# The late modulation's pieces of the head passes on GpSimd instead of VectorE

## The reference

```python
def _adaln(cvec, w_mod, b_mod):
    m = jax.nn.silu(cvec) @ w_mod + b_mod                # (2048) @ (2048, 6 * 2048)
    return jnp.split(m[..., None, :], 6, axis=-1)        # shift, scale, gate of mixer and FFN

def _block(s, mod, s0_f, s0_b, p):
    sh_a, sc_a, g_a, sh_f, sc_f, g_f = mod
    h = _rmsnorm(s, p['norm_pre_mix']) * (1.0 + sc_a) + sh_a
    out, s_f, s_b = _mixer(h, s0_f, s0_b, p)             # 8 heads of gated DeltaNet | Hyena
    s = s + g_a * _rmsnorm(out, p['norm_post_mix'])
    h = _rmsnorm(s, p['norm_pre_ffn']) * (1.0 + sc_f) + sh_f
    ff = (jax.nn.silu(h @ p['w_gate']) * (h @ p['w_up'])) @ p['w_down']
    return s + g_f * _rmsnorm(ff, p['norm_post_ffn']), s_f, s_b
```

## Time and profile before

| | us |
|---|---|
| median of three runs | 1667.03 |
| the runs | 1659.72, 1667.03, 1667.48 |
| the profiled execution | 1659.05 |
| its span, from first to last instruction | 1657.4 |
| TensorE busy | 1608.8 |
| VectorE busy | 1148.5 |
| ScalarE busy | 769.1 |
| GpSimd busy | 117.1 |

### The profile page before, as it was taken

The page is one execution under the profiler, slowest core; times in us unless marked ns, Lnnn a source line. Parts: engine busy times, 40 slices in busy tenths (PEclk is TensorE's granted clock), DMA queues, the critical chain, the costliest instruction groups (busy, mean ns, idle before and its releaser), DMA issues.

```text
span 1657.4 us, 26938 instructions
## 1 busy us (share of the span) xinstructions
PE 1608.8 (97%) x10074; PEld 1398.9 (84%) x10074; DVE 1148.5 (69%) x1699; ACT 769.1 (46%) x1285; POOL 117.1 (7%) x214
## 2 busy tenths in 40 slices
PE   6998999999999999999998999999999999999997
PEld 2356999999998998999998888888888888888886
DVE  4726889899898997776777555555555555655665
ACT  3436465564646556433346444444444444343331
POOL 1001010110101010000110000000000000111110
PEclk9998999999999999999999999999999999999999
DMA  9996354453544545324993444554455446877872
GB/s 367 414 356 237 121 166 153 134 179 121 172 138 132 171 133 185 102 102 154 342 330 140 152 182 175 200 202 175 180 202 198 172 187 242 283 247 253 281 250 93
DMA packets 83067, 332.59 MB, mean 201 GB/s; under 512 B 8073, under 2 KB 24538, under 8 KB 56668
## 3 DMA queue, kind: packets, MB, share of 16 engines
q1 hardware_dynamic: 63168, 262.44, 43.1%
q0 software_dynamic: 19408, 67.77, 12.3%
q10 hardware_dynamic: 396, 1.10, 0.2%
HBM read 327.09 MB, written 4.19 MB: 200 GB/s over the span
## 4 chain that ended last, share of the span: by engine, by line
PE 82%; DMA 8%; DVE 5%; ACT 2%; DVEq 1%; issue 1%; SPq 0%; ACTq 0%
PE g L490 10%; PE o L490 10%; PE o L483 7%; PE o L484 7%; PE o L485 7%; PE g L491 5%; PE o L491 5%; DMA w_mod_tile_o<-in_w_mod_t 4%; DMA w_mod_raw<-in_w_mod_t 4%; PE g L566 2%; PE o L497 2%; PE g L497 2%; PE o L499 2%; PE g L499 2%; PE g L498 2%; PE g L577 2%
## 5 line engine op out<-in xcount | busy, mean ns | idle before, releaser
L464 DVE TENSOR_TENSOR w_lo<-w_raw,w_hi 128x2048 fp32r<-128x2048 f32 x202 | 462.4, 2289 | 201.8 <-ACT w_hi L459 201.4
L459 ACT CAST w_hi<-w_raw 128x2048 fp32r<-128x2048 f32 x203 | 388.0, 1911 | 219.3 <-PE o L499 73.9
L483 PE MATMUL o<-h_hi,w_hi 128*128 128x256 f32 (+1 forms) x880 | 291.6, 331 | 2.3 <-ACT hy_x L1232 1.3
L485 PE MATMUL o<-h_hi,w_lo 128*128 128x256 f32 (+1 forms) x880 | 275.3, 313 | 0.0
L484 PE MATMUL o<-h_lo,w_hi 128*128 128x256 f32 (+1 forms) x880 | 275.1, 313 | 0.0
L490 PE MATMUL g<-h_hi_lo,w_hi 128*128 128x512 f32 x704 | 245.0, 394 | 0.0
L490 PE MATMUL o<-h_hi_lo,w_hi 128*128 128x512 f32 x688 | 240.5, 394 | 2.0 <-DVE h_hi_lo L2036 2.0
L491 PE MATMUL g<-h_hi_lo,w_lo 128*128 128x256 f32 x704 | 195.0, 277 | 0.0
L491 PE MATMUL o<-h_hi_lo,w_lo 128*128 128x256 f32 x688 | 190.6, 277 | 0.0
L483 PEld LDWEIGHTS o<-h_hi,w_hi 128*128 128x128 f32 x880 | 168.0, 191 | 13.6 <-issue 6.9
L485 PEld LDWEIGHTS o<-h_hi,w_lo 128*128 128x128 f32 x880 | 167.4, 190 | 10.4
(11 more groups left out here) (393 smaller groups left out, 2820.1 us busy)
## 6 DMA issues: line engine op xcount, KB each, us to landing
w_raw<-in_w_ff_t SPq DMA_DIRECT2D x88, 1024.0 KB, 6.1
w_raw<-in_w_heads_t SPq DMA_DIRECT2D x56, 1024.0 KB, 4.9
w_mod_raw<-in_w_mod_t SPq DMA_DIRECT2D x32, 1024.0 KB, 11.1
w_raw<-in_w_down_t SPq DMA_DIRECT2D x32, 1024.0 KB, 6.8
w_mod_piece_h<-in_w_mod_t POOLq DMA_DIRECT2D x112, 256.0 KB, 3.6
w_raw<-in_w_out_t SPq DMA_DIRECT2D x16, 1024.0 KB, 8.4
w_mod_tile_o<-in_w_mod_t POOLq DMA_DIRECT2D x16, 1024.0 KB, 9.8
w_mod_piece_d<-in_w_mod_t POOLq DMA_DIRECT2D x64, 256.0 KB, 5.9
```

Source lines behind the costliest of these rows:

```text
L459: e.copy(whi[p.split[j]][:], raw[p.raw[j]][:]).then_inc(hi_ready, 1)
L464: e.tensor_tensor(wlo[p.split[j]][:], raw[p.raw[j]][:], whi[p.split[j]][:].bitcast(F32), ALU.subtract).then_inc(lo_ready, 1)
L483: e.matmul(o, a, xh, start=first, stop=False)
L485: return e.matmul(o, b, xh, start=False, stop=last)
```

## The change

VectorE's `head_pieces` and its 16 places in the order of a pass go. GpSimd's `head_load` becomes `head_chunk`: it waits until the column sum of the pass before is done (`macc_used`), then goes through the pieces, issuing the load of piece n and computing piece n - 2. VectorE's one instruction (multiply by a column and add) becomes two on GpSimd: `tensor_scalar` in place in the piece's buffer, then `tensor_tensor` into `w_mod_sum_h`, with a drain before each. The loop over pass pairs on GpSimd is written out as straight code. The pieces of the later stages stay on VectorE, and the orders of TensorE, ScalarE and SyncE are the same.

```diff
--- before.py
+++ after.py
@@ -1503,13 +1503,6 @@
             else:
                 last = v.tensor_scalar(acc, raw_, c, None, mulv)
             last.then_inc(mtile_done, 1)
-
-        def head_pieces(v, pairs, u, k0, k1):
-
-            for k in range(k0, k1):
-                v.drain()
-                v.wait_ge(mpiece_landed[piece_slot(u, k)], piece_landed(pairs, u, k))
-                mod_piece(v, k, mpiece_h[piece_slot(u, k)][:], macc_h[:])
 
         def out_pieces(v, t0, t1):
 
@@ -1887,9 +1880,6 @@
                     if not (isinstance(g, int) and g == 0):
                         scan_dve_(v, g - 1, 1 - u, step)
 
-                def pc(k0, k1):
-                    head_pieces(v, 0 if p is Hf else i + 1 - u, u, k0, k1)
-
                 def mod():
                     modulation(v, g + 5, 1, g + 1, F[1])
 
@@ -1898,12 +1888,12 @@
                         v.wait_ge(rows_t, 9)
                         v.tensor_tensor(modc[:, 0, 48:52], F[1][:, 0:8:2], bmod[:, 48:52], addv)
 
-                inv("hv"); pc(0, 1); scan("v0"); pc(1, 3); late_row(); rp(); scan("S0"); pc(3, 4); scan("v1"); pc(4, 5); scan("w1"); pc(5, 6)
-                inv("nr"); scan("S1"); pc(6, 7); inv("kt"); inv("bb"); scan("v2"); pc(7, 9); scan("w2"); cc(); pc(9, 10); inv("A")
-                scan("v3"); inv("U0"); pc(10, 11); inv("D1"); inv("ag"); scan("S2"); inv("M1"); pc(11, 12); inv("DT1"); scan("w3")
+                inv("hv"); scan("v0"); late_row(); rp(); scan("S0"); scan("v1"); scan("w1")
+                inv("nr"); scan("S1"); inv("kt"); inv("bb"); scan("v2"); scan("w2"); cc(); inv("A")
+                scan("v3"); inv("U0"); inv("D1"); inv("ag"); scan("S2"); inv("M1"); inv("DT1"); scan("w3")
                 cv(0); inv("M2"); inv("DT2"); re(0); inv("D2"); scan("nb"); inv("M3"); inv("DT3"); re(1); at_(); inv("D3")
-                inv("M4"); cv(1); inv("DT4"); re(2); cv(2); inv("D4"); sm(0); pc(12, 13); inv("M5"); inv("DT5"); re(3); pc(13, 14)
-                inv("D5"); sm(1); inv("M6"); pc(14, 15); inv("DT6"); pc(15, 16); cv(4); re(4); inv("D6"); sm(2); scan("mix")
+                inv("M4"); cv(1); inv("DT4"); re(2); cv(2); inv("D4"); sm(0); inv("M5"); inv("DT5"); re(3)
+                inv("D5"); sm(1); inv("M6"); inv("DT6"); cv(4); re(4); inv("D6"); sm(2); scan("mix")
                 cv(5); mod(); zm(); inv("Z")
                 v.drain()
 
@@ -2111,12 +2101,27 @@
             def piece(n, k):
                 return A["w_mod_t"][4 * n + k // 4][:, k % 4 * 512:(k % 4 + 1) * 512]
 
-            def head_load(h, u):
-
-                for k in range(16):
-                    wait_count(g, mtile_done, 16 * h + k + 1 - piece_gap(u, k))
-                    s = piece_slot(u, k)
-                    g.dma_start(mpiece_h[s][:], piece(13 + h, k)).then_inc(mpiece_landed[s], 16)
+            def head_chunk(h, u, pairs):
+
+                wait_count(g, macc_used, h)
+                for n in range(18):
+                    if n < 16:
+                        wait_count(g, mtile_done, 16 * h + n + 1 - piece_gap(u, n))
+                        s = piece_slot(u, n)
+                        g.dma_start(mpiece_h[s][:], piece(13 + h, n)).then_inc(mpiece_landed[s], 16)
+                    k = n - 2
+                    if k >= 0:
+                        s = piece_slot(u, k)
+                        g.drain()
+                        g.wait_ge(mpiece_landed[s], piece_landed(pairs, u, k))
+                        c = cvec[:, 2, 2 * k:2 * k + 1]
+                        if k:
+                            g.tensor_scalar(mpiece_h[s][:], mpiece_h[s][:], c, None, ALU.mult)
+                            g.drain()
+                            last = g.tensor_tensor(macc_h[:], macc_h[:], mpiece_h[s][:], ALU.add)
+                        else:
+                            last = g.tensor_scalar(macc_h[:], mpiece_h[s][:], c, None, ALU.mult)
+                        last.then_inc(mtile_done, 1)
 
             g.memset(fm[FW:P, 0], 0.0)
             g.memset(fw[FW:P, 3 * FW:], 0.0).then_inc(filt_pad, 1)
@@ -2144,10 +2149,10 @@
             g.dma_start(lev[:].bitcast(F32), A["c_lev"]).then_inc(lev_in, 16)
             g.wait_ge(first_used, 4)
             g.wait_ge(w_used, st.tile(H0, 0, 1) + 1)
-            head_load(0, 0)
-            with g.Fori(0, H.iters) as i:
-                head_load(2 * i + 1, 1)
-                head_load(2 * i + 2, 0)
+            head_chunk(0, 0, 0)
+            for i in range(H.iters):
+                head_chunk(2 * i + 1, 1, i)
+                head_chunk(2 * i + 2, 0, i + 1)
             w_ov(g, HEADS - 1, "mix")
             by_pairs = A["w_mod_t"].rearrange("(c g) p (h f) -> g h p c f", g=4, h=2)
             for t in range(16):
```

## The result

The changed kernel takes 1964.82 us (median of four runs, 1951.64 to 1970.37) against 1666.3 before: ratio 1.1797, 95% interval 1.1756 to 1.1838. It is slower, as forecast, but by 299 us and not by 50, and outside the range. Ratios leave out one execution of 5670.66 us, in `early_seven` further down; the median of its nine runs has it in. The page after, to set against the earlier trace rows: span, busy time and share by engine, and the granted clock in 40 slices.

A forecast was written before the change was run, and what follows sets the result against it. TensorE was taken to bound the head passes. VectorE's loss of 9.2 us, less 0.75 and 1.3, gave 7.2 us a pass; seven passes, 50 us, on 1659.05 made 1709 us, range 1655 to 1760.

The forecast's parts named there:

- A piece then takes 3.9 us: GpSimd's time per piece in the head passes: 3.2 us, plus 0.7 us of waiting for VectorE's two-tile instructions.
- two more steps of 0.30: In GpSimd's time per piece: two steps from a semaphore to the start, 0.30 us each, beside issue and arithmetic.
- The scaling: GpSimd's in-place scaling of a 512-element piece: two memory streams, between 0.45 and 0.90 us, taken as 0.68.
- the addition: GpSimd's addition of a piece into the sum: three memory streams, 0.75 to 1.35 us, taken as 1.05.
- rival C: Head passes become as long as GpSimd's chain, the column sum waiting for the sixteenth piece: up to 1761 us; chance 0.17.
- threshold of 4.2 us: Time per piece in a head pass, (70.57 - 3.6) / 16, from which the column sum waits for GpSimd's sixteenth piece.
- other sign: What would show rival C in a pass besides TensorE idle before L512: GpSimd has no gaps.
- the forecast's own high end: Late stretch of a pass: 4.4 us a piece, 15.2 us held and all lost; 13.1 us a pass, +92, 1751.
- What bounds the kernel: In the head passes TensorE is busy 70.57 of 70.57 us; relieving VectorE of 11.8 us a pass is worth 0.
- Exclusion between the engines: GpSimd arithmetic holds up VectorE instructions reading two tiles: 9.2 us lost, 7.2 us a pass after slack, 50 in all.
- The place: Loss counts late in the pass, 386.07 to 415.74, where VectorE sheds few pieces; earlier, twelve removed pieces cover it.
- rival D: TensorE gains from earlier operands, at the tail (2.9 us) and at bank changes: 14.5 us in all, 1645; chance 0.05.

The follow-up runs named there:

- early_seven: Changed kernel without GpSimd drains, its arithmetic kept for pieces 0 to 7 of a pass and left out for 8 to 15: 1677.45 us, ratio 1.0053.
- the late run: Changed kernel without GpSimd drains, its arithmetic kept for pieces 8 to 14 and the first scaling, held back until the inversion's first level: 1708.08 us, ratio 1.0244.

## Why the prediction was wrong, and where it was right

- **The step that failed**: "A piece then takes 3.9 us", under the 4.2 us from which GpSimd is the bound. It took 6.9. The term mis-sized is the "two more steps of 0.30" for the drains: I took them for a step of the queue, and the first lasts until the transfer just issued has landed, 2.9 to 3.1 us. The 3.6 us from issue to landing stood in the earlier trace rows, and I had used it only for the piece that the transfer brings. Of 6.9 us the two drains take 3.05 and 0.17 where I had 0.60. The scaling was off too (1.56 for 0.68 us), the addition less (1.26 for 1.05). By themselves these two would not have made GpSimd the bound: without drains it waits for TensorE.
- **The prediction's rival C (GpSimd becomes the bound) was what happened**, and its first sign was right (TensorE in front of L512, behind the sixteenth piece). Its threshold of 4.2 us fits: at 4.3 us a piece, with memsets, TensorE begins to wait, 3.6 us in all. Its price was wrong: 1761 at most, 1965 measured, since it used the same steps. Its other sign was wrong: I had GpSimd without gaps, and it stands idle in its drains for 3 us a piece. And the forecast's own high end, 4.4 us a piece, already lay above the 4.2 from which rival C holds, so I had not kept the two apart.
- **What bounds the kernel**: right. A pass was at TensorE's pace, and VectorE's relief alone is worth nothing (0.9989 with the arithmetic left out).
- **Exclusion between the engines**: right, and by the forecast's size: 8.5 us a pass in the kernel without drains, against 7.2. That the sizes are so near is in part luck. The loss on VectorE is 18.4 us a pass, 11.8 of it made good by the removed pieces; GpSimd holds for 2.8 us a piece and not 1.73; and 128-column scalings are held too, which I had not counted. By the Trainium skill (SBUF — State Buffer, section Who interferes with whom) a VectorE instruction with two SBUF inputs contends with a GpSimd instruction that reads SBUF, and not with one that only writes it. The traces here agree: the masks take 942 ns beside a GpSimd that reads, against 687, and 685 beside one that writes.
- **The place**: right. Late in the pass 6.5 us for seven pairs, early 1.6, which I had put at nothing. The path was only in part the one I had named: TensorE's wait for VectorE's D in front of L577 (L578 there) is 3.7 us over the late run's six passes, and its wait for ScalarE's D in front of L572 (L573 there) is 19.3.
- **TensorE gains (the prediction's rival D)**: no. In the run with transfers and no arithmetic the 2.9 us at the tail did not go away with the pieces, and the longer products at a change of bank stayed (296 and 424 ns, 294 and 424 before).

## What to carry to other kernels

Price a drain on GpSimd behind a transfer that it issued by that transfer's time to landing, not as a step of the queue. Order GpSimd's own instructions with a semaphore that they raise, which gave back 241 of 299 us here; to issue the transfers from ScalarE gave back 220, and made ScalarE wait. Work moved to GpSimd is not free because GpSimd's share is small: look at its chain from the wait that starts it to the wait that ends it, and at what VectorE reads beside it, in the stretch in which VectorE has nothing to give. And relief of an engine that nobody waits for is worth nothing, at 91% of busy time too.

## What the runs showed that I had not expected

- A drain on GpSimd behind its own transfer lets the next instruction start 0.1 to 0.6 us after landing: 6.0, 9.0 and 11.0 us behind the issue for transfers of 1 MB that landed after 5.9, 8.8 and 10.4.
- GpSimd takes 1.56 us to scale 128 x 512 values in place and 1.25 to add two tiles of that size; a memset of it takes 0.53.
- Without a drain behind the issue, arithmetic starts 0.04 us after it: the issue itself does not stand in its way.
